# Slot entries of the expert blocks: one load from the DRAM table and an on-chip copy, in place of two loads

## The chip, the cores and the metric

The kernel runs on one core of a Trainium2 chip. The metric is device time in microseconds of one whole execution: one program that computes a decoder layer for a prompt of 1,040 rows and a sample group of 64 rows. Before the change the median of 3 runs is 2792.64 us (2786.09 to 2794.36).

A core has five engines with queues of their own: PE (TensorE, matmuls), DVE (VectorE), ACT (ScalarE), POOL (GpSimd) and SP (SyncE, which only issues DMAs here). They meet through semaphores. DMAs issued by SP travel in queue q1, those issued by POOL (the indirect ones) in queue q0; both are worked off by the same 16 DMA engines.

## The reference

The layer ends in a mixture of experts. That part, cut to what matters:

```python
scores = sigmoid(x @ router_w)
_, idx = top_k(scores + router_bias, 8)              # 8 of 64 experts for each of the 1,104 rows
gate = take(scores, idx); gate = gate / sum(gate) * 2.5
for e in range(64):                                  # rows grouped by expert
    xb = x[rows_of_expert_e]                         # gather
    y = (silu(xb @ w_exp_gate[e]) * (xb @ w_exp_up[e])) @ w_exp_down[e]   # 1024 -> 256 -> 1024
    out[rows_of_expert_e] += y * gate                # scatter with accumulation
```

Everything before it (latent attention, a gated recurrence, the merge, the router, the shared expert) and the final norm are untouched by the change.

## The kernel before, in words

Work is cut into stages; the change lies in `stage_experts`, which fills the last 1,100 us of the run. The router stage has written a table in DRAM: one entry of two words (the row's number and its routing weight) for each slot, 192 slots (`CAP`) to a block. One block is one expert with up to 192 rows; the loop runs over pairs of blocks, s = 0 (called even here) and s = 1 (odd), 64 blocks in all. Nearly every buffer exists twice, one for each s.

For block n each engine does this:

- **SP** loads the entries of a block (`entries`, L1830) and its three weight matrices (`weights`, L1834), gate, up and down, 1 MB each. Everything is loaded two blocks ahead, into the buffers that block n is leaving. A block's entries are loaded twice: into `gi` for block n+2 (L1852), once the gather of block n has landed (L1851), and into `si` for block n itself (L1857), once the scatter of block n-2 has landed (L1856). Between the two stand the weight loads of block n+2, each behind a wait for DVE's `part_weights` of the same matrix of block n (L1854). That of GATE stands near the start of DVE's block n-1, that of UP near its end, that of DOWN at the start of DVE's block n.
- **POOL** gathers rows (`gather`, L1867): two indirect DMAs of 96 rows of 4 KB each, with the row numbers in `gi`; and scatters results (`scatter`, L1875), two indirect DMAs that add into DRAM, with the row numbers in `si`. Its order is: gather n+2, scatter n, gather n+3, wait until scatter n has landed, scatter n+1, wait until scatter n+1 has landed. It signals `si_free` after each of the two landings. So the gather for an even block stands behind the landing of the odd scatter before it; that for an odd block stands behind no landing.
- **ACT** rounds weights and gathered rows to their high parts (L1992, L1997), does the sigmoid, and writes the results scaled by the routing weight (`part`, L1999, which reads `si`; its first part of a block waits for `si`, L2003).
- **DVE** takes the low parts (`part_weights`, L2046 to L2048; `part_quarter`, L2050 to L2053) and does the products of the gate. Its block n begins with `part_weights` of DOWN for block n and of GATE for block n+1.
- **PE** does the gate and up products of block n, then transposes the gathered rows of block n+1 (`turn`, L1907, first transposes of a block wait for `xg_in`, the landed gather) between the down products of block n.

The two places at which the routing data can hold up PE are therefore the transposes of block n+1 (L1916), which need the gathered rows, and the first `part` of block n (L2005), which needs `si`: the down products stop when the banks aren't emptied.

The waits of the functions quoted below decide the order; nothing is planned by a scheduler.

Of the kernel before, what the change touches and what calls it, by code (L numbers as in the profile page):

```python
# [8 lines left out]
I32 = mybir.dt.int32  # L9
# [32 lines left out]
CAP = 192  # L42
HALF = CAP // 2
# [1740 lines left out]
def stage_experts(nc, S, I, O):  # L1784
    arena, split, PS, sem = S.arena, S.split, S.psum, S.sem
# [8 lines left out]
    xr = split.take(2, 2 * KD, HALF)  # L1794
    hr = split.take(2, 2, CAP + 128 - HALF)
    raw_in = [[sem(f"e_{n}{s}") for s in range(2)] for n in ("wg", "wu", "wd")]
    gi_in, si_in, xg_in, y_out = ([sem(f"e_{n}{s}") for s in range(2)] for n in ("gi", "si", "xg", "yo"))
    rounded, parted = ([sem(f"e_{n}{j}") for j in range(3)] for n in ("hi", "lo"))
    xr_full, xr_rounded, xr_parted = sem("e_xrf"), sem("e_xrh"), [sem("e_xrl0"), sem("e_xrl1")]
    gate_full, up_full, sig_ready, gated, h_made, h_ready = (sem("e_" + n) for n in ("gf", "uf", "sg", "gg", "hm", "hr"))  # L1800
    gate_half, up_half, gate_ready, up_ready = (sem("e_" + n) for n in ("gh", "uh", "gr", "ur"))
    part_full, part_copied, zeros = sem("e_pf"), sem("e_pc"), sem("e_zero")
    si_free = [sem("e_sf0"), sem("e_sf1")]
    passed = sem("e_passed")
    GBANK, UBANK, DBANK = (2, 3), (4, 5), (6, 7)
    HI, LO = 0, 1
# [13 lines left out]
    @block.sync  # L1820
    def _(sp):
        last = last_pair(sp)

        def first_slot(n):
            return sp.value_load(S.blocks_i[0:1, 1, bass.ds(n, 1)], min_val=0, max_val=SLOTS - CAP)

        def expert(n):
            return sp.value_load(S.blocks_i[0:1, 0, bass.ds(n, 1)], min_val=0, max_val=EXPERTS - 1)

        def entries(dst, sems, s, first):  # L1830
            sp.dma_start(dst[0:HALF, s].rearrange("p (h w) -> p h w", h=2).bitcast(I32),
                         S.table[bass.ds(first, CAP)].rearrange("(h p) w -> p h w", p=HALF)).then_inc(sems[s], 16)

        def weights(s, j, e):  # L1834
            name = ("w_exp_gate", "w_exp_up", "w_exp_down")[j]
            src = I[name][bass.ds(e, 1)].rearrange("a p n -> p (a n)")
            sp.dma_start(raw[:, s, j], src).then_inc(raw_in[j][s], 16)

        for s in range(2):
            entries(gi, gi_in, s, first_slot(s))  # L1840
        for s in range(2):
            for j in range(3):
                if s == 0 and j == 1:
                    sp.wait_ge(xg_in[0], 32)
                weights(s, j, s)
        with sp.Fori(0, last) as it:
            first = [first_slot(2 * it + s) for s in range(4)]
            e = [expert(2 * it + 2 + s) for s in range(2)]
            for s in range(2):
                n = 2 * it + s  # L1850
                sp.wait_ge(xg_in[s], 32 * (it + 1))  # L1851
                entries(gi, gi_in, s, first[2 + s])  # L1852
                for j in range(3):
                    sp.wait_ge(parted[j], n + 1)  # L1854
                    weights(s, j, e[s])
                sp.wait_ge(si_free[s], it + 1)  # L1856
                entries(si, si_in, s, first[s])  # L1857
        ends = [first_slot(2 * last + s) for s in range(2)]
        for s in range(2):
            sp.wait_ge(si_free[s], last + 1)  # L1860
            entries(si, si_in, s, ends[s])

    @block.gpsimd
    def _(pool):
# [10 lines left out]
        def scatter(s, turn):  # L1875
            if s:
                pool.wait_ge(y_out[0], 32 * (turn + 1))
                pool.sem_inc(si_free[0], 1)
            pool.wait_ge(part_copied, 4 * (2 * turn + s) + 8)
            pool.sem_inc(passed, 1)  # L1880
            for hf in range(2):
                pool.indirect_dma_start(out=S.y_dram, in_=y[0:HALF, s, hf], in_offset=None, compute_op=ALU.add,  # L1882
                                        out_offset=bass.IndirectOffsetOnAxis(ap=si[0:HALF, s, 2 * hf:2 * hf + 1].bitcast(I32), axis=0)
                                        ).then_inc(y_out[s], 16)
# [102 lines left out]
    def _(act):  # L1987
# [11 lines left out]
        def part(s, turn_, p):  # L1999

            hf, c = p // 2, p % 2
            if p == 0:
                act.wait_ge(si_in[s], 16 * (turn_ + 1))  # L2003
            act.wait_ge(part_full, 4 * (2 * turn_ + s) + p + 1)
            act.activation(y[0:HALF, s, hf, 512 * c:512 * (c + 1)], PS[0:HALF, DBANK[c]], ACT.Copy,  # L2005
                           scale=si[0:HALF, s, 2 * hf + 1:2 * hf + 2]).then_inc(part_copied, 1)
# [36 lines left out]
    def _(dve):  # L2043
        last = last_pair(dve)

        def part_weights(s, turn_, j):  # L2046
            dve.wait_ge(rounded[j], 2 * turn_ + s + 1)
            dve.tensor_tensor(wr[:, s, j, LO], raw[:, s, j], wr[:, s, j, HI].bitcast(F32), ALU.subtract).then_inc(parted[j], 1)  # L2048

        def part_quarter(s, turn_, r):  # L2050
            hf, g = r // 2, r % 2
            dve.wait_ge(xr_rounded, 4 * (2 * turn_ + s) + r + 1)
            dve.tensor_tensor(quarter(xr[:, LO], hf, g), bank4(g), quarter(xr[:, HI], hf, g).bitcast(F32), ALU.subtract).then_inc(xr_parted[g], 1)  # L2053

        def body(it, ends):
            for s in range(2):
                n = 2 * it + s
                nxt = (1, it) if s == 0 else (0, it + 1)
                more = not (ends and s)
                part_weights(s, it, DOWN)  # L2060
                if more:
                    part_weights(*nxt, GATE)
# [123 lines left out]
class State:  # L2186
# [11 lines left out]
    def sem(self, name):  # L2198
        self.sems.append(self.nc.alloc_semaphore(name))
        return self.sems[-1]  # L2200
# [176 lines left out]
```

## Time and profile before

| | us |
|---|---|
| median of 3 runs | 2792.64 |
| the profiled execution | 2795.52 |
| its span, first to last instruction | 2793.7 |
| PE busy | 2474.0 (89%) |
| DVE busy | 1362.5 (49%) |
| ACT busy | 1044.8 (37%) |
| POOL busy | 579.3 (21%) |
| q1 (SP's DMAs), share of 16 engines over the span | 27.3% |
| q0 (POOL's DMAs), share of 16 engines over the span | 18.1% |

How to read it: shares over the whole span mix stages with different limits. The stage of the change is read from the slices and timelines of its own stretch, about 1643 to 2730 us. A block of that stage is recognised by one instruction that occurs once in it, the sigmoid (ACT, L2018); the distance of two of them is the block's period. A timeline row gives start, duration, engine, line, operation, output and input, and in brackets the idle time before it with what ended it. A row that ends in x2 merges two instructions: its duration reaches from the start of the first to the end of the second, with the wait between them. GpSimd's rows for an indirect DMA are the time it takes to write and issue it, not the transfer.

### The profile page before, as it was taken

To read this page: it belongs to the slowest core of one execution; us is meant where nothing else is said; L and a number is where in the kernel's file an instruction comes from. 1 tells how busy PE (TensorE), PEld (TensorE's weight loads), DVE (VectorE), ACT (ScalarE), POOL (GpSimd) and SP (SyncE) were. 2 spreads that over 40 slices of the span, in tenths; PEclk is the share of its full clock that TensorE was granted. 3 is DMA by queue.
4 is the path that set the end of the run, shared out by engine and by line. 5 is a ranking of instruction groups with operands and counts; after the bars stand their busy time and mean duration, and the time that the engine had idled before them with its cause. 6 is when DMAs were issued, how large, how long until landed. Compare 5 with 4: busy or idle time off the path is not lost. (4 is left out here: it accounts for less than half of the span.)

```text
span 2793.7 us, 36499 instructions
## 1 busy us (share of the span) xinstructions
PE 2474.0 (89%) x13126; PEld 1851.2 (66%) x13126; DVE 1362.5 (49%) x2701; ACT 1044.8 (37%) x1662; POOL 579.3 (21%) x452
## 2 busy tenths in 40 slices
PE   8888888899966679999998669999999999999990
PEld 4455556564455646666454448999989999989990
DVE  0545544200066601011266137777777777777764
ACT  1145533200023100000021026666666766666652
POOL 0020022000000000000035103344433444344423
PEclk9989989999999889999999889999999999999995
DMA  3000043210010040100113069999999999999964
GB/s 131 0 12 1 1 154 151 87 38 0 0 41 0 0 170 23 45 23 23 51 31 112 15 233 271 287 282 285 287 285 285 298 287 287 273 292 281 284 176 155
DMA packets 113752, 395.23 MB, mean 141 GB/s; under 512 B 41590, under 2 KB 50886, under 8 KB 85254
## 3 DMA queue, kind: packets, MB, share of 16 engines
q1 hardware_dynamic: 78390, 269.63, 27.3%
q0 software_dynamic: 35296, 124.70, 18.1%
q8 instruction: 44, 0.72, 0.1%
q14 instruction: 22, 0.18, 0.0%
HBM read 325.74 MB, written 69.13 MB: 141 GB/s over the span
## 5 line engine op out<-in xcount | busy, mean ns | idle before, releaser
L1934 PE MATMUL banks<-split 128*128 128x384 f32 x1792 | 538.2, 363 | 0.0
L2048 DVE TENSOR_TENSOR split<-rest,split 128x2048 fp32r<-128x2048 f32 x192 | 438.8, 2286 | 108.2 <-ACT split L1992 91.4
L1932 PE MATMUL banks<-split 128*128 128x192 f32 x2048 | 482.7, 256 | 0.0
L1954 PE MATMUL banks<-split 128*128 128x512 f32 x1536 | 406.8, 407 | 17.3 <-ACT rest L2005 14.6
L1932 PEld LDWEIGHTS banks<-split 128*128 128x128 f32 x2048 | 389.1, 192 | 2.7
L1992 ACT CAST split<-rest 128x2048 fp32r<-128x2048 f32 x192 | 359.3, 1904 | 65.0 <-DMA rest<-in_w_exp_gate 60.1
L1393 PE MATMUL banks<-big 128*128 128x368 f32 x1152 | 358.9, 475 | 14.5 <-DMA big<-in_w_merge 14.5
L1934 PEld LDWEIGHTS banks<-split 128*128 128x128 f32 x1792 | 338.9, 189 | 0.0
L1882 POOL DMA_INDIRECT y_rows<-rest x128 | 266.7, 2083 | 336.5 <-ACT rest L2005 299.0
L1954 PEld LDWEIGHTS banks<-split 128*128 128x128 f32 x1536 | 276.5, 190 | 71.9 <-ACT rest L2005 17.5
L1393 PEld LDWEIGHTS banks<-big 128*128 128x128 f32 x1152 | 220.0, 191 | 153.1 <-issue 17.0
L2005 ACT ACTIVATE rest<-banks,rest 96x512 f32<-96x512 f32 x256 | 175.7, 687 | 215.1 <-PE banks L1954 166.2
L1871 POOL DMA_INDIRECT rest<-x_rows,rest x128 | 163.0, 1273 | 414.7 <-issue 298.2
L1486 POOL DMA_INDIRECT slot_table<-big x72 | 69.3, 963 | 526.0 <-DVE big L1648 506.5
L1413 DVE TENSOR_TENSOR big<-big,banks 128x368 f32<-128x368 f32 x24 | 12.9, 537 | 328.0 <-ACT big L1403 328.0
L2053 DVE TENSOR_TENSOR split<-banks,split 128x384 fp32r<-128x384 f32 x256 | 131.5, 550 | 17.8 <-ACT split L1997 17.5
L1402 ACT ACTIVATE big<-banks 128x368 f32<-128x368 f32 x24 | 11.5, 477 | 341.1 <-PE banks L1393 341.1
L177 PE MATMUL banks<-big 128*128 128x368 f32 (+1 forms) x354 | 115.4, 488 | 23.9 <-DMA big<-in_w_cols 13.9
L1916 PE MATMUL banks<-base,rest 96*128 96x96 f32 x1024 | 117.9, 248 | 18.4 <-DMA rest<-x_rows,rest 17.8
L1916 PEld LDWEIGHTS banks<-base,rest 96*128 96x128 f32 x1024 | 106.9, 142 | 40.1 <-DMA rest<-x_rows,rest 17.7
L995 PE MATMUL banks<-big 128*128 128x368 f32 x384 | 121.4, 480 | 7.7 <-DMA big<-in_w_cols 7.7
L1499 PE MATMUL banks<-big 128*128 128x512 f32 (+1 forms) x288 | 125.3, 594 | 2.9 <-PEq L2220 2.9
(327 smaller groups left out, 3088.0 us busy)
## 6 DMA issues: line engine op xcount, KB each, us to landing
rest<-in_w_exp_gate SPq DMA_DIRECT2D x64, 1024.0 KB, 9.1
rest<-in_w_exp_up SPq DMA_DIRECT2D x64, 1024.0 KB
rest<-in_w_exp_down SPq DMA_DIRECT2D x64, 1024.0 KB, 7.1
big<-in_w_merge SPq DMA_DIRECT2D x8, 1536.0 KB, 6.3
big<-in_w_cols SPq DMA_DIRECT2D x11, 512.0 KB, 3.8
x_rows<-big SPq DMA_DIRECT2D x9, 512.0 KB
y_rows<-big SPq DMA_DIRECT2D x9, 512.0 KB, 2.6
big<-in_x_cols SPq DMA_DIRECT2D x3, 1472.0 KB, 17.7
```

The source lines that it names most:

```text
L1393: ins = pe.matmul(PS[:, 4 * (u % 2) + b, 0:CH], w[:, s, at + j], src[:, j, cols], start=(j == 0), stop=(j == k - 1))
L1499: ins = pe.matmul(PS[0:r, 2 * (i % 2) + c], S.merged[:, k, 128 * i:128 * i + r], wout[:, k, 512 * c:512 * (c + 1)], start=(k == 0), stop=( ...
L1871: pool.indirect_dma_start(out=xg[0:HALF, s, hf], out_offset=None, in_=S.x1_dram, in_offset=bass.IndirectOffsetOnAxis(ap=gi[0:HALF, s, 2 * ...
L1882: pool.indirect_dma_start(out=S.y_dram, in_=y[0:HALF, s, hf], in_offset=None, compute_op=ALU.add, out_offset=bass.IndirectOffsetOnAxis(ap= ...
L1916: ins = pe.transpose(PS[:, g, HALF * k:HALF * (k + 1)], xg[0:HALF, s, hf, 512 * g + 128 * k:512 * g + 128 * (k + 1)], S.ident[0:HALF, 0:HALF])
L1932: ins = pe.matmul(PS[:, banks[f], 0:CAP], wr[:, s, j, LO, at:at + 128], x[:, k, 0:2], start=False, stop=False)
L1934: ins = pe.matmul(PS[:, banks[f], 0:2 * CAP], wr[:, s, j, HI, at:at + 128], x[:, k], start=False, stop=(k == KD - 1))
L1954: ins = pe.matmul(PS[:, DBANK[c]], hr[:, a, f, HALF * hf:HALF * hf + 128], wr[:, s, DOWN, b, at:at + 512], start=(f == 0 and j == 0), stop ...
L1992: act.copy(wr[:, s, j, HI], raw[:, s, j]).then_inc(rounded[j], 1)
L2005: act.activation(y[0:HALF, s, hf, 512 * c:512 * (c + 1)], PS[0:HALF, DBANK[c]], ACT.Copy, scale=si[0:HALF, s, 2 * hf + 1:2 * hf + 2]).then ...
L2048: dve.tensor_tensor(wr[:, s, j, LO], raw[:, s, j], wr[:, s, j, HI].bitcast(F32), ALU.subtract).then_inc(parted[j], 1)
L2053: dve.tensor_tensor(quarter(xr[:, LO], hf, g), bank4(g), quarter(xr[:, HI], hf, g).bitcast(F32), ALU.subtract).then_inc(xr_parted[g], 1)
```

## The change

The second load of the entries, with its semaphores `si_in`, goes: 64 loads inside the loop and after it. In its place DVE copies `gi` to `si` (`keep_entries`), two copies of 96x2 words (row numbers as integers, routing weights as floats), at the start of its block n, ahead of `part_weights` of DOWN. The copies wait until the gather of block n has landed and until `si_free` says that the scatter of block n-2 has. They signal `si_made`. SP's load of the next entries into `gi` now waits for `si_made` of block n in place of `xg_in`, since the copy reads `gi`. ACT's first part and POOL's scatter wait for `si_made` as well.

```diff
             for s in range(2):
                 n = 2 * it + s
-                sp.wait_ge(xg_in[s], 32 * (it + 1))
-                entries(gi, gi_in, s, first[2 + s])
+                sp.wait_ge(si_made[s], 2 * (it + 1))
+                entries(s, first[s])
                 for j in range(3):
                     sp.wait_ge(parted[j], n + 1)
                     weights(s, j, e[s])
-                sp.wait_ge(si_free[s], it + 1)
-                entries(si, si_in, s, first[s])
-        ends = [first_slot(2 * last + s) for s in range(2)]
-        for s in range(2):
-            sp.wait_ge(si_free[s], last + 1)
-            entries(si, si_in, s, ends[s])
...
         def scatter(s, turn):
             if s:
                 pool.wait_ge(y_out[0], 32 * (turn + 1))
                 pool.sem_inc(si_free[0], 1)
+            pool.wait_ge(si_made[s], 2 * (turn + 1))
             pool.wait_ge(part_copied, 4 * (2 * turn + s) + 8)
...
             if p == 0:
-                act.wait_ge(si_in[s], 16 * (turn_ + 1))
+                act.wait_ge(si_made[s], 2 * (turn_ + 1))
...
+        def keep_entries(s, turn_):
+            dve.wait_ge(xg_in[s], 32 * (turn_ + 1))
+            dve.wait_ge(si_free[s], turn_ + 1)
+            kept, loaded = (v[0:HALF, s].rearrange("p (h w) -> p h w", h=2) for v in (si, gi))
+            dve.tensor_copy(kept[:, :, 0].bitcast(I32), loaded[:, :, 0].bitcast(I32)).then_inc(si_made[s], 1)
+            dve.tensor_copy(kept[:, :, 1], loaded[:, :, 1]).then_inc(si_made[s], 1)
+
         def body(it, ends):
             for s in range(2):
                 n = 2 * it + s
                 nxt = (1, it) if s == 0 else (0, it + 1)
                 more = not (ends and s)
+                keep_entries(s, it)
                 part_weights(s, it, DOWN)
```

What stands in SP's queue for one block of the loop, before the change (L1831 is the load of entries, first into `gi`, last into `si`; ISA and REGISTER_ALU rows compute addresses and wait values):

```order
L1851 ISA
L1831 ISA
L1831 DMA rest<-slot_table 96x2x2
L1854 REGISTER_ALU
L1837 ISA
L1837 DMA rest<-in_w_exp_gate 128x2048
L1837 DMA rest<-in_w_exp_up 128x2048
L1837 DMA rest<-in_w_exp_down 128x2048
L1831 ISA
L1831 DMA rest<-slot_table 96x2x2
```

And with it:

```order
L1851 ISA
L1831 ISA
L1831 DMA rest<-slot_table 96x2x2
L1854 REGISTER_ALU
L1837 ISA
L1837 DMA rest<-in_w_exp_gate 128x2048
L1837 DMA rest<-in_w_exp_up 128x2048
L1837 DMA rest<-in_w_exp_down 128x2048
```

The last load is gone; the three weight loads keep their place behind the first load of entries, whose wait (L1851) is now one for DVE.

DVE's queue from the end of one block (`part_quarter`, `part_weights` UP) into the next (`part_weights` DOWN and GATE, then the products of the gate), before:

```order
L2053 TENSOR_TENSOR split<-banks,split 128x384
L2048 TENSOR_TENSOR split<-rest,split 128x2048
L2047 ISA
L2048 TENSOR_TENSOR split<-rest,split 128x2048
L2064 TENSOR_TENSOR rest<-rest,banks 128x384
```

And with the change (the lines behind it have moved on by numbers only: L2053 is now L2048, L2048 is L2043, L2064 is L2067):

```order
L2048 TENSOR_TENSOR split<-banks,split 128x384
L2054 COPY rest<-rest 96x2
L2055 COPY rest<-rest 96x2
L2043 TENSOR_TENSOR split<-rest,split 128x2048
L2042 ISA
L2043 TENSOR_TENSOR split<-rest,split 128x2048
L2067 TENSOR_TENSOR rest<-rest,banks 128x384
```

Two copies stand between the blocks, ahead of both weight parts.

## Rows read from the trace of the kernel before

**Rows 1.** The page, parts 1 and 2: busy time of the engines, DMA share by slice.

```profile
PE 2474.0 (89%) x13126; PEld 1851.2 (66%) x13126; DVE 1362.5 (49%) x2701; ACT 1044.8 (37%) x1662; POOL 579.3 (21%) x452
...
DMA  3000043210010040100113069999999999999964
```

**Rows 2.** Waits, 1200 to 2750 us: who waited for whom, total, times, longest us.

```profile
ACT rest L2005 <- DMA rest<-slot_table: 48.8, 16, 5.0
...
PE banks L1916 <- DMA rest<-x_rows,rest: 17.8, 5, 16.8
```

**Rows 3.** Timeline of ScalarE: start us, duration us, group, [idle before <- releaser].

```profile
1672.37 0.52 ACT L2018 ACTIVATE rest<-rest 128x384 f32<-128x384 f32 x1 [0.62 <-issue]
...
2072.58 0.53 ACT L2018 ACTIVATE rest<-rest 128x384 f32<-128x384 f32 x1 [0.62 <-DVE rest L2064]
...
2080.53 0.68 ACT L2005 ACTIVATE rest<-banks,rest 96x512 f32<-96x512 f32 x1 [3.24 <-DMA rest<-slot_table]
...
2090.08 0.53 ACT L2018 ACTIVATE rest<-rest 128x384 f32<-128x384 f32 x1 [0.62 <-DVE rest L2064]
...
2106.29 0.53 ACT L2018 ACTIVATE rest<-rest 128x384 f32<-128x384 f32 x1 [0.62 <-DVE rest L2064]
...
2715.76 0.53 ACT L2018 ACTIVATE rest<-rest 128x384 f32<-128x384 f32 x1 [0.62 <-DVE rest L2064]
```

**Rows 4.** Windows, the stretch 1700 to 2700 us: busy by engine, PEclk, DMA share, GB/s.

```profile
1700.00:2700.00 1000.00, 986.15 (x6296) 911.72 (x6295) 750.66 (x1026) 686.76 (x908) 410.29 (x241) 1.00 0.95 283
```

**Rows 5.** Timeline of SyncE's queue, one odd block (start us, duration us).

```profile
2114.74 0.35 SPq L1837 DMA_DIRECT2D rest<-in_w_exp_up  x1
2117.87 0.33 SPq L1837 DMA_DIRECT2D rest<-in_w_exp_down  x1
2118.39 7.22 SPq L1831 DMA_DIRECT2D rest<-slot_table  x2
2126.02 0.19 SPq L1837 DMA_DIRECT2D rest<-in_w_exp_gate  x1
```

**Rows 6.** Timeline of GpSimd, around the same pair, and one earlier gather.

```profile
2049.71 2.65 POOL L1871 DMA_INDIRECT rest<-x_rows,rest  x1 [9.28 <-issue]
...
2102.09 1.47 POOL L1882 DMA_INDIRECT y_rows<-rest  x1 [8.84 <-ACT rest L2005]
2103.86 2.88 POOL L1882 DMA_INDIRECT y_rows<-rest  x1 [0.30 <-issue]
2115.39 0.94 POOL L1871 DMA_INDIRECT rest<-x_rows,rest  x1 [8.65 <-issue]
2116.64 2.01 POOL L1871 DMA_INDIRECT rest<-x_rows,rest  x1 [0.30 <-issue]
```

**Rows 7.** Timeline of TensorE: the first transposes in that odd block.

```profile
2125.83 0.82 PE L1916 MATMUL banks<-base,rest 96*128 96x96 f32 x8
```

**Rows 8.** DMA view, 2114 to 2150 us in 40 slices of 0.9 us.

```profile
GB/s 0 55 91 437 419 337 346 373 419 323 287 246 205 201 214 237 351 256 228 214 369 378 401 437 400 428 437 392 205 205 366 364 350 296 228 0 0 55 127 391
```

**Rows 9.** Timeline of VectorE: the two weight parts at a block's start.

```profile
2115.56 2.28 DVE L2048 TENSOR_TENSOR split<-rest,split 128x2048 fp32r<-128x2048 f32 x1
2119.32 2.29 DVE L2048 TENSOR_TENSOR split<-rest,split 128x2048 fp32r<-128x2048 f32 x1 [1.47 <-ACT split L1992]
```

**Rows 10.** Groups by line and form, VectorE: a small integer copy in SBUF.

```profile
L1646 DVE COPY big<-big 128x8 int32<-128x8 int32 x8 | 1.3, 167 | 0.0
```

**Rows 11.** Line 1882 (scatter), 2000 to 2200 us: from issue to landing.

```profile
DMA to landing us min/median/max: 7.2/9.2/10.8
```

**Rows 12.** DMA queues, 1674 to 1678 us: packets, MB, share of 16 engines.

```profile
q1 hardware_dynamic: 137, 0.89, 66.7%
q0 software_dynamic: 120, 0.45, 34.7%
```

**Rows 13.** DMA queues, 2120 to 2122.5 us.

```profile
q1 hardware_dynamic: 107, 0.88, 91.9%
q0 software_dynamic: 32, 0.07, 10.7%
```

More of the change, by code:

```diff
@@ L1796, in stage_experts @@
     raw_in = [[sem(f"e_{n}{s}") for s in range(2)] for n in ("wg", "wu", "wd")]
-    gi_in, si_in, xg_in, y_out = ([sem(f"e_{n}{s}") for s in range(2)] for n in ("gi", "si", "xg", "yo"))
+    gi_in, xg_in, y_out = ([sem(f"e_{n}{s}") for s in range(2)] for n in ("gi", "xg", "yo"))
     rounded, parted = ([sem(f"e_{n}{j}") for j in range(3)] for n in ("hi", "lo"))
@@ L1802, in stage_experts @@
     part_full, part_copied, zeros = sem("e_pf"), sem("e_pc"), sem("e_zero")
-    si_free = [sem("e_sf0"), sem("e_sf1")]
+    si_free, si_made = [sem("e_sf0"), sem("e_sf1")], [sem("e_sm0"), sem("e_sm1")]
     passed = sem("e_passed")
@@ L1828, in expert, with entries @@
             return sp.value_load(S.blocks_i[0:1, 0, bass.ds(n, 1)], min_val=0, max_val=EXPERTS - 1)
-        def entries(dst, sems, s, first):
-            sp.dma_start(dst[0:HALF, s].rearrange("p (h w) -> p h w", h=2).bitcast(I32),
-                         S.table[bass.ds(first, CAP)].rearrange("(h p) w -> p h w", p=HALF)).then_inc(sems[s], 16)
+        def entries(s, first):
+            sp.dma_start(gi[0:HALF, s].rearrange("p (h w) -> p h w", h=2).bitcast(I32),
+                         S.table[bass.ds(first, CAP)].rearrange("(h p) w -> p h w", p=HALF)).then_inc(gi_in[s], 16)
         def weights(s, j, e):
@@ L1839, in _ @@
         for s in range(2):
-            entries(gi, gi_in, s, first_slot(s))
+            entries(s, first_slot(s))
         for s in range(2):
@@ L1846, in _ @@
         with sp.Fori(0, last) as it:
-            first = [first_slot(2 * it + s) for s in range(4)]
+            first = [first_slot(2 * it + 2 + s) for s in range(2)]
             e = [expert(2 * it + 2 + s) for s in range(2)]
```

## The prediction

> **What bounds the kernel now.** I read the page first: PE is busy 89% of the span, and in the last third of the slices the DMA engines stand at 9 of 10 as well [rows 1]. So the expert stage has two candidates, and an average does not choose between them. Next the period of a block, from the sigmoid that occurs once in each. The 64 blocks lie between 1672.37 and 2715.76: 63 periods in 1043.4 us, 16.56 each. An undisturbed period is 2106.29 - 2090.08 = 16.21 [rows 3], and in such a one PE has no gap. 63 x 16.21 is 1021.2, so all stalls of the stage together cost 22.2 us. That is the most the change can win in the loop.
>
> The waits name what makes them. ACT's first part waited for the slot entries 16 times, 48.8 us; PE's transposes waited for gathered rows 5 times, 17.8 us, of which 16.8 is the first gather of the stage [rows 2]. The first is what a long block looks like: at 2080.53 ACT had waited 3.24 us for `si`, and that period is 17.50 [rows 3]. ACT idles there some 1.6 us anyway for PE's down products, which is why 48.8 us of waiting are only about 20 us of delay: 22.2 less the 2 that I give to late gathers (1.0 on PE's own row, the rest is what the late rows did to ACT and DVE behind it, an estimate).
>
> Last, the share of the DMA engines over a thousand microseconds of the stage: 0.95 [rows 4]. There is next to no slack in transfers either, so it matters which one stands ahead of which.
>
> **What goes.** The load of `si` stood last in q1, behind three weight loads; with the copy the entries are on chip before the block begins. That takes the 16 waits: -20 us. The load itself is 192 entries of 8 bytes; SP needs about 0.4 us to issue it and is not the bound. No term.
>
> **What is added.** Two DVE copies of 96x2 words. The nearest row is an integer copy of 128x8 in 167 ns [rows 10]: 0.33 us a block. DVE idles 1.47 us before the second weight part of each block, waiting for ACT [rows 9], which covers them: 0. Without cover it would be 64 x 0.33 = 21 us. The new wait for `si_free` stands on DVE with everything of the block behind it. The scatter that it waits for landed at latest just before the gather at 2115.39 [rows 6], DVE comes at 2115.56 [rows 9]: 0.2 us to spare, while landing takes 7.2 to 10.8 us [rows 11]. Up to 1.47 us late is swallowed by the same idle time. I take 0 and keep what lies beyond it as a rival.
>
> **What is moved, and the term that decides.** In SP's queue the gate and up loads stand behind the load into `gi`, and that now waits for DVE's start of block n. Both parts they also wait for (GATE and UP of block n) are done by then, so SP issues entries, gate and up in one go. Before, the gate load of the odd block's queue came at 2126.02 and that of the even one earlier in its block; now it comes together with up, just where up alone stood. Nothing that needs these weights suffers: ACT rounds them a whole block (16 us) later, and at 437 GB/s [rows 8] 1 MB takes 2.4 us.
>
> But look at what else is issued there. The gather for the next even block stands behind the landing of the odd scatter and goes out at 2115.39 and 2116.64 (the second half until 2118.65) [rows 6]. It is back at about 2125.2: SP's pair of entry loads ends at 2125.61 [rows 5], and the second of them waited for it. PE wants the rows at 2125.83 [rows 7]. The margin is 0.6 us in an undisturbed pair; it is this kernel's second critical path, with nothing to show for itself but those few waits of [rows 2].
>
> Now the engines' work in that gap. Before: up (issued 2114.74, first bytes a good microsecond later, done about 2118.3 [rows 5, 8]), first half, down (2117.87), second half. That down goes ahead of the second half is in 2120 to 2122.5: 91.9% for q1, 10.7% for q0 [rows 13]. Changed: DVE is through the copies at 2115.9, SP issues entries at 2116.0, gate at 2116.5, up at 2117.0; gate's bytes run from 2117.7 to 2120.1. The first half comes behind gate instead of behind up, 1.8 us later, and the second behind up instead of down. So the rows land 1.8 us later, less the margin: PE stalls 1.2 us in each pair. If instead gather and weights share packet by packet from 2118.3 on, the 192 packets of 4 KB pass with as many of 8 KB beside them: 1.57 MB at 437 GB/s are 3.6 us, 0.79 MB at 356 (the slice of rows 8 in which weights and rows are mixed) are 2.2, end at 2124.1. Counted in the same way, before ended at 2115.9 + 2 x 2.4 + 2.2 = 2122.9 and landed 2.3 later; with 1.2 to 2.3 for that the rows land at 2125.3 to 2126.4, and the stall is 0 to 0.6. That both queues run at once does occur: 66.7% and 34.7% between 1674 and 1678 [rows 12], with a deep backlog in q1. Bounds 0 and 1.2; I take 0.8, nearer the upper since the order in rows 13 is from the very place.
>
> The Trainium skill, DMA: Bandwidth & Descriptors, section Queues, rings and completion order, says that each DMA engine "round-robins between the queue rows it has work for, at packet granularity". By that the gather gets in after at most one packet of weights and never stands behind the whole backlog; rows 12 agree, and rows 13 show that the turn can be as long as one weight load. Without the rule, first come first served, the stall would be that of the last rival below.
>
> In some pairs it is worse. In 10 of 30 pairs the first half of the even gather takes 2.4 to 3.0 us to issue in place of 0.94, as at 2049.71 [rows 6]: it starts after DVE's long subtraction has begun and ends after it. Then both halves come some 2 us later. Before, they found the queue nearly empty; now gate and up are both in front, and rows 13's order makes it 1.8 to 2.5 us more on a margin that is already gone. I take 2.2, bounds 1.8 and 2.6.
>
> The Trainium skill, SBUF — State Buffer, section Who interferes with whom, has the reason: a DVE instruction with two SBUF inputs contends with a GpSimd one that reads SBUF, and who issues first holds the port for the whole instruction. The 2.65 us against 0.94 agree. The copies move the subtraction 0.3 us back, which by that rule would let a few more first halves through; it is not counted.
>
> The sum over 31 pairs: 2/3 x 0.8 + 1/3 x 2.2 = 1.27 us, times 31 = 39 us. These stalls include what late gathers cost now, so the stage goes from 22.2 us of stalls to 39: +17. The profiled execution took 2795.52, 2.9 over the median; the difference goes on the median: 2792.64 + 17 = 2810.
>
> **Rivals.** *The wait goes and nothing takes its place.* For it: the gather shares the engines packet by packet; the gate load no longer runs between the two halves of the odd scatter, which might land, and so start the gather, a microsecond earlier. Against: weights issued before that scatter fill the same place. Stalls fall to 0 to 3 us: 2792.6 - 20 = 2773. It decides if the gather lands before 2125.8 on the clock of the rows, that is loses less than 0.6 us.
>
> *The gain is handed back evenly:* 0.7 us a pair, 22 us: 2793. This is the case between, where the rows land 1 us later in the plain pairs and the late third loses little more.
>
> *DVE's new wait becomes the chain.* Three weight loads and the even scatter share the engines, the scatter lands more than 1.5 us after DVE's arrival and DVE drags the gate products. For it: 0.2 us to spare. Against: where PE already stalls for the gather, the scatter gains the same time. With 3 us late in every second block, 1.5 on the path: 31 x 1.5 = 47 on top of the 39, less 22: 2857.
>
> *First come, first served:* the second half behind gate, up and down, 2117.7 + 3 x 2.4 + 2.2 = 2127.1 and 1.2 to land, 2128.3, 2.5 us too late in each pair: 78 - 22 = +56: 2849.
>
> *The change doesn't do what it says:* only if `si_free` came so late that entries are again last. Then the stall sits on DVE, which is the third case.
>
> **How the numbers follow.** Late gathers, net loss: 0.42, centre 2810, its own range 2798 to 2830. Wait gone, no new one: 0.33, 2773. Even: 0.15, 2793. DVE's chain 0.05, first come first served 0.05. About 0.3% (8 us) is what a measurement of this kernel can tell from no change. Faster by more than that: 0.35; within: 0.17; slower: 0.48. The range has to take in most of the second case, whose end is 2771, and the upper half of the first with the 2.6 of the late pairs: 2771 to 2840.
>
> **What would show it.** Right: no wait of ACT L2005 for entries; SP's entries, gate and up within 1.5 us of each other at each block start; PE L1916 waiting for gathered rows in most odd blocks, about 1 us each and 30 to 40 us in all; even blocks at 16.2. Wrong: L1916 waits of under 10 us in total (then the second case), or a DVE copy idle for more than 1.5 us before it with gate products late (the DVE case). If the period of the undisturbed pair itself changed, some engine's cost was missed.

## The result: 3.7% slower, and the profile after

| us | before | after |
|---|---|---|
| median (6 runs each) | 2790.32 | 2893.45 |
| lowest to highest | 2782.00 to 2794.36 | 2882.04 to 2898.45 |
| ratio after/before, 95% interval | | 1.0369 [1.0344, 1.0394] |
| span of the profiled execution | 2793.7 | 2887.3 |

The forecast was 2810 with a range up to 2840. The direction, slower, came true; the size did not: +103 us, not +17.

The page after, parts 1 and 2, the rows that answer to [rows 1]:

```profile
PE 2505.3 (87%) x13126; PEld 1874.9 (65%) x13126; DVE 1378.2 (48%) x2829; ACT 1048.6 (36%) x1662; POOL 587.1 (20%) x452
...
DMA  3000042200100310101130488888888888888764
```

PE's work is the same 13126 instructions, yet it is busy 31 us longer. The DMA digits of the expert stage fell from 9 to 8: the transfers of the stage are spread over more time.

Waits of after, 1200 to 2950 us (total, times, longest), the rows that answer to [rows 2]:

```profile
PE banks L1911 <- DMA rest<-x_rows,rest: 100.5, 31, 16.2
...
DVE rest L2054 <- POOLq L1872: 6.5, 13, 0.6
```

ACT's wait for `slot_table` is not in the list any more (48.8 us in [rows 2]). PE's wait for gathered rows, 17.8 us over 5 times before, is 100.5 us over 31. L1911 is the line of the transposes now. The second row is the copies' wait for `si_free`.

ScalarE after: the sigmoid that opens the measure of the stage, a plain even block, a long odd one, a plain even one, a short odd one, and the last, to be laid beside [rows 3]:

```profile
1664.66 0.52 ACT L2013 ACTIVATE rest<-rest 128x384 f32<-128x384 f32 x1 [0.62 <-DVE rest L2067]
...
2131.52 0.53 ACT L2013 ACTIVATE rest<-rest 128x384 f32<-128x384 f32 x1 [0.62 <-DVE rest L2067]
...
2147.73 0.53 ACT L2013 ACTIVATE rest<-rest 128x384 f32<-128x384 f32 x1 [0.62 <-DVE rest L2067]
...
2155.97 0.48 ACT L1992 CAST split<-banks 128x384 fp32r<-128x384 f32 x1 [4.40 <-PE banks L1911]
...
2169.85 0.53 ACT L2013 ACTIVATE rest<-rest 128x384 f32<-128x384 f32 x1 [0.62 <-DVE rest L2067]
...
2186.06 0.53 ACT L2013 ACTIVATE rest<-rest 128x384 f32<-128x384 f32 x1 [0.62 <-DVE rest L2067]
...
2191.19 0.86 ACT L1992 CAST split<-banks 128x384 fp32r<-128x384 f32 x2 [1.28 <-PE banks L1911]
...
2809.73 0.53 ACT L2013 ACTIVATE rest<-rest 128x384 f32<-128x384 f32 x1 [0.62 <-DVE rest L2067]
```

From the first to the last sigmoid it is 1145.1 us, against 1043.4 before. 63 undisturbed periods are still 1021.2, so the stalls grew from 22.2 to 123.9 us: +101.7, and nothing outside the stage grew (it begins 7.7 us earlier in this execution of after; the first sigmoid of the kernels below lies anywhere from 1659 to 1679). The even period is 2147.73 - 2131.52 = 16.21. The odd one that follows is 22.12, with ACT idle for 4.40 us because the transposes had not filled its banks.

I split blocks 2 to 63 (counted from 0) by their period, each sigmoid less 5.78 us, which puts a block's edge near its start. All even ones take 16.2. Of the 30 odd ones from block 3 to 61, 17 are long (21.95 to 23.98, mean 22.66) and 13 short (17.09 to 17.65, mean 17.30). The long ones carry 17 x 6.45 = 110 us, the short ones 13 x 1.09 = 14. Every short one follows a long one, and all but three of the long ones after the first follow a short one.

SyncE's queue after, at the start of the long block and of the short one (to be laid beside [rows 5]):

```profile
2141.16 0.33 SPq L1831 DMA_DIRECT2D rest<-slot_table  x1
2141.74 0.33 SPq L1837 DMA_DIRECT2D rest<-in_w_exp_gate  x1
...
2143.22 0.33 SPq L1837 DMA_DIRECT2D rest<-in_w_exp_down  x1
...
2179.49 0.33 SPq L1831 DMA_DIRECT2D rest<-slot_table  x1
2180.07 0.33 SPq L1837 DMA_DIRECT2D rest<-in_w_exp_gate  x1
...
2181.55 0.33 SPq L1837 DMA_DIRECT2D rest<-in_w_exp_down  x1
```

Entries, gate, up (between the two rows of L1837) and down, 3 MB, leave within 2.1 us, where [rows 5] had up, down and gate 3 and 8 us apart. GpSimd over the same two pairs (beside [rows 6]):

```profile
2141.77 2.24 POOL L1865 DMA_INDIRECT rest<-x_rows,rest  x1 [9.81 <-issue]
2144.32 0.93 POOL L1865 DMA_INDIRECT rest<-x_rows,rest  x1 [0.30 <-issue]
...
2178.98 0.94 POOL L1865 DMA_INDIRECT rest<-x_rows,rest  x1 [8.71 <-issue]
2180.23 2.11 POOL L1865 DMA_INDIRECT rest<-x_rows,rest  x1 [0.30 <-issue]
```

The first two rows are the even gather of the long pair: it starts at 2141.77, after SP has issued gate, and takes 2.24 us for its first half. In the short pair it starts at 2178.98, before SP has issued anything, and its first half takes 0.94.

TensorE in the long block, first transposes (beside [rows 7]):

```profile
2155.31 1.26 PE L1911 MATMUL banks<-base,rest 96*128 96x96 f32 x8 [4.10 <-DMA rest<-x_rows,rest]
```

The DMA queues of after from 2146 to 2151 us, and from 2151 to 2155:

```profile
q1 hardware_dynamic: 187, 1.36, 75.1%
q0 software_dynamic: 117, 0.42, 25.1%
...
q0 software_dynamic: 156, 0.57, 53.8%
q1 hardware_dynamic: 95, 0.65, 51.3%
```

The gather's 192 packets run from 2147.3 to 2154.4, beside the backlog of weights. Sorted by microsecond, the trace's packet records show 26 to 32 row packets and 18 to 29 of weights in most of them, packet for packet. Behind the weights, at 2158, 84 row packets (those of the next gather) pass in one. The 192 packets of the gather take 7.1 us. In the ten pairs of before whose first half was held, with at most 12 packets of weights left beside them, 192 rows took 2.8 to 3.0 us.

The gather also starts late behind the weights. The queues from 2144 to 2147 us, just after its first half has left GpSimd in the long pair, and from 2180.6 to 2182 in the short pair:

```profile
q1 hardware_dynamic: 168, 1.25, 99.1%
...
q0 software_dynamic: 70, 0.28, 82.3%
```

In the long pair the first row packet comes 3.3 us after the end of that issue, while weights alone pass; in the short pair, where no weights are on their way yet, 0.7 us after it. By the packet records it is 3.1 to 3.4 us in all 17 long pairs, behind 157 to 176 packets of weights, and 0.7 to 0.8 in the 13 short ones.

Windows after, two pairs of blocks and then the idle of the long block (each engine's busy us and count in the order PE, PEld, DVE, ACT, POOL; granted clock; DMA share; GB/s):

```profile
2125.70:2141.90 16.20, 16.20 (x106) 15.04 (x105) 12.77 (x20) 11.40 (x15) 4.47 (x3) 1.00 0.81 251
2141.90:2164.10 22.20, 18.10 (x106) 16.37 (x105) 13.29 (x20) 11.43 (x15) 9.33 (x6) 0.92 0.82 248
2164.10:2180.30 16.20, 16.20 (x105) 15.03 (x105) 12.12 (x20) 11.39 (x15) 5.35 (x4) 1.00 0.78 243
2180.30:2197.80 17.50, 16.44 (x106) 15.03 (x105) 12.52 (x20) 11.35 (x15) 7.71 (x5) 1.00 1.00 305
...
2151.00:2156.00 5.00, 0.90 (x8) 0.70 (x7) 1.34 (x4) 0.42 (x3) 1.45 (x2) 0.97 1.05 285
2156.00:2160.00 4.00, 4.00 (x17) 3.24 (x16) 3.31 (x3) 0.94 (x3) 0.00 (x0) 0.62 1.04 263
2160.00:2164.00 4.00, 4.00 (x23) 3.29 (x22) 2.50 (x5) 2.72 (x5) 0.00 (x0) 1.00 0.12 28
```

The long block is 6.0 us longer than the plain one. 4.10 of it is PE's idle time; the other 1.90 is PE's own work, 18.10 us for matmuls that take 16.20 otherwise: in the 4 us after the idle the granted clock is 0.62, a mean of the two levels 1.2 and 2.4 GHz. After the idle of the short block, 1.1 us, the clock stays at 1.00. The DMA engines, full at 2151 to 2160, are all but empty at 2160 to 2164 (0.12): the transfers of a block come in one heap.

### The profile page after: what moved, and what is told of

It reads as the page before. It is cut to its first block and busy times, and to the rows that moved or that the text cites. A ratio compares the mean times of both kernels' runs of the same rounds, so it can differ in the third digit from the quotient of the medians.

```text
span 2887.3 us, 36338 instructions
## 1 busy us (share of the span) xinstructions
PE 2505.3 (87%) x13126; PEld 1874.9 (65%) x13126; DVE 1378.2 (48%) x2829; ACT 1048.6 (36%) x1662; POOL 587.1 (20%) x452
## 5 line engine op out<-in xcount | busy, mean ns | idle before, releaser
L2043 DVE TENSOR_TENSOR split<-rest,split 128x2048 fp32r<-128x2048 f32 x192 | 439.0, 2286 | 98.1 <-ACT split L1987 98.1
L1949 PE MATMUL banks<-split 128*128 128x512 f32 x1536 | 429.9, 425 | 2.5 <-DVE split L2075 2.4
L1927 PEld LDWEIGHTS banks<-split 128*128 128x128 f32 x2048 | 389.2, 192 | 2.7
L1393 PE MATMUL banks<-big 128*128 128x368 f32 x1152 | 358.4, 474 | 15.5 <-DMA big<-in_w_merge 15.5
L1929 PEld LDWEIGHTS banks<-split 128*128 128x128 f32 x1792 | 339.0, 189 | 0.0
L1949 PEld LDWEIGHTS banks<-split 128*128 128x128 f32 x1536 | 294.1, 202 | 60.1 <-DVE split L2075 2.8
L1865 POOL DMA_INDIRECT rest<-x_rows,rest x128 | 172.4, 1347 | 415.1 <-issue 299.5
L1911 PE MATMUL banks<-base,rest 96*128 96x96 f32 x1024 | 128.8, 263 | 101.0 <-DMA rest<-x_rows,rest 100.5
L1911 PEld LDWEIGHTS banks<-base,rest 96*128 96x128 f32 x1024 | 113.6, 151 | 128.5 <-issue 93.1
L2048 DVE TENSOR_TENSOR split<-banks,split 128x384 fp32r<-128x384 f32 x256 | 134.5, 551 | 106.5 <-ACT split L1992 104.9
L1992 ACT CAST split<-banks 128x384 fp32r<-128x384 f32 x256 | 116.3, 474 | 100.5 <-PE banks L1911 99.9
```

What stands on the lines that cost most here:

```text
L1393: ins = pe.matmul(PS[:, 4 * (u % 2) + b, 0:CH], w[:, s, at + j], src[:, j, cols], start=(j == 0), stop=(j == k - 1))
L1865: pool.indirect_dma_start(out=xg[0:HALF, s, hf], out_offset=None, in_=S.x1_dram, in_offset=bass.IndirectOffsetOnAxis(ap=gi[0:HALF, s, 2 * ...
L1911: ins = pe.transpose(PS[:, g, HALF * k:HALF * (k + 1)], xg[0:HALF, s, hf, 512 * g + 128 * k:512 * g + 128 * (k + 1)], S.ident[0:HALF, 0:HALF])
L1927: ins = pe.matmul(PS[:, banks[f], 0:CAP], wr[:, s, j, LO, at:at + 128], x[:, k, 0:2], start=False, stop=False)
L1929: ins = pe.matmul(PS[:, banks[f], 0:2 * CAP], wr[:, s, j, HI, at:at + 128], x[:, k], start=False, stop=(k == KD - 1))
L1949: ins = pe.matmul(PS[:, DBANK[c]], hr[:, a, f, HALF * hf:HALF * hf + 128], wr[:, s, DOWN, b, at:at + 512], start=(f == 0 and j == 0), stop ...
```

## The experiments

The stage is always the stretch from its first to its last sigmoid (1043.4 before, 1145.1 after). "Row waits" are those of PE's transposes for gathered rows.

### e1: the copies stay, entries go third

```diff
-                sp.wait_ge(si_made[s], 2 * (it + 1))
-                entries(s, first[s])
                 for j in range(3):
+                    if j == DOWN:
+                        sp.wait_ge(si_made[s], 2 * (it + 1))
+                        entries(s, first[s])
                     sp.wait_ge(parted[j], n + 1)
```

> The changed kernel, with SyncE's order inside a block altered: gate and up loads first, each behind its own old wait, then the load of entries behind the copies, then down. The copies on DVE and their waits stay. Theory A (the gather for the even block shares the DMA engines with gate and up, issued together just before it): up goes out again at 14.2 us of a block and gate near 5, the gather lands as in the kernel before, PE waits under 10 us for rows in the loop, no wait for entries: 2765 to 2785 us, faster than before. Theory B (the copies and the wait for si_free in DVE's queue make the loss): DVE's queue is untouched, so it stays near 2890. Theory C (the load of entries itself comes too late for the gather that needs it): it comes even later here, so 2890 or more, with GpSimd waiting for slot_table.

2780.73 us, ratio to before 0.9968 [0.9952, 0.9984]; stage 1032.3.

```profile
PE banks L1912 <- DMA rest<-x_rows,rest: 21.8, 8, 16.7
```

The copies and DVE's new wait are all still here, and the loss is gone: it is the order in SP's queue. With gate and up back at their old places the change is a small gain. The even gather starts late here as well, in 17 of 30 pairs later than 15.1 us of its even block, as in this one (16.1 us):

```profile
2064.61 2.16 POOL L1866 DMA_INDIRECT rest<-x_rows,rest  x1 [9.92 <-issue]
```

Yet the odd block behind this one takes 16.31, and 14 of the 17 take 16.2 to 16.7 (the others 17.2, 17.3 and 20.0). With gate and up through before it, a late gather alone does not make a long block.

### e2: the kernel before, its gate load held back to the up load's place

```diff
-                    sp.wait_ge(parted[j], n + 1)
+                    sp.wait_ge(parted[UP if j == GATE else j], n + 1)
```

> The kernel before, two loads of entries, no copies; only SyncE's gate load waits for DVE's low part of UP in place of that of GATE, so gate and up go out together at the end of a block. Theory A: most of the loss is here without any copy: long waits of PE for gathered rows in odd blocks, half-speed clock behind the longest, 2850 to 2900 us, and the waits for entries remain or vanish in them. Theory B and theory C: near 2790.

2896.16, ratio 1.0400 [1.0365, 1.0435]; stage 1150.1.

```profile
ACT rest L2005 <- DMA rest<-slot_table: 149.4, 32, 5.7
...
PE banks L1916 <- DMA rest<-x_rows,rest: 26.2, 11, 15.6
```

The loss is as large, but by another way: `si`, still loaded last, is late in every second block, and the row waits hardly grow. So it shows that a heap of loads costs whoever stands behind it, and says little on the gather.

### e5: e1 with the gate load beside the up load

The same edit of the wait as in e2, in e1.

> As e1_entries_third (copies, entries loaded third, 2780.7 us), but the gate load waits for DVE's low part of UP, so gate goes out with up at 14.3 us of a block instead of at 5. The only difference to e1 is when 1 MB is issued. Theory A (bytes of weights beside the gather and the scatter that it follows): PE waits for gathered rows in all odd blocks, 2870 to 2900 us. Rival D (the changed kernel lost by loading up 1 to 2 us later, behind DVE's copies, not by the gate load): up is as early as in the kernel before, so 2780 to 2795 us.

2817.68, ratio 1.0096 [1.0072, 1.0120]; stage 1076.2; row waits 47.5 us, 13 times. That lies between what the two theories gave. Gate's place alone makes 44 us of stage against e1. The rest to after (69 us) comes with the entries in front of gate and up, which puts both behind DVE's copy and so beside the even gather.

### e4: the copies behind part_weights of DOWN

```diff
-                keep_entries(s, it)
                 part_weights(s, it, DOWN)
+                keep_entries(s, it)
```

> The changed kernel, with the copies one instruction later on DVE, behind the low part of DOWN. All three weight loads then go out together at about 1.4 us of a block, 2.5 us later than in the changed kernel, and the even gather gets ahead of them. Theory A: the gather lands in time, PE's waits for rows fall below 20 us, 2765 to 2800 us, unless the three loads now hold up the scatter, which the next gather stands behind. Theory B (DVE's copies and wait are the cost): the wait for si_free is 2.5 us shorter, gain of the 6 us that DVE waits for it at most: 2885. Theory C: the entries come 2.5 us later still: 2890 or more.

2918.71, ratio 1.0468 [1.0437, 1.0499]; stage 1173.4; row waits 115.8 us, 31 times. I was wrong, and the caveat in the text came true. From issue to landing of the scatters, 2000 to 2300 us, before ([rows 11] is the same line over a shorter stretch), after, e1 and e4:

```profile
DMA to landing us min/median/max: 7.2/9.5/10.8
```

```profile
DMA to landing us min/median/max: 9.7/10.6/12.5
```

```profile
DMA to landing us min/median/max: 6.5/9.6/11.8
```

```profile
DMA to landing us min/median/max: 10.1/12.3/12.7
```

The heap now runs beside the odd scatter, whose landing starts the even gather; that start moves to 0.9 us into the odd block, and the odd blocks take 21.1 to 21.8, all but three of them. This half of the matter was not in my sum: the weights delay the gather's start as well as its packets.

### e3 and e11: what GpSimd's long issue costs

e3 splits the subtraction of DOWN into two halves of 1.21 us, back to back:

```diff
+            if j == DOWN:
+                dve.tensor_tensor(wr[:, s, j, LO, 0:DM], raw[:, s, j, 0:DM], wr[:, s, j, HI, 0:DM].bitcast(F32), ALU.subtract)
+                dve.tensor_tensor(wr[:, s, j, LO, DM:], raw[:, s, j, DM:], wr[:, s, j, HI, DM:].bitcast(F32), ALU.subtract).then_inc(parted[j], 1)
+                return
```

> The changed kernel, with DVE's low part of DOWN as two subtractions of 1024 columns. In 16 of 31 pairs the first half of the even gather takes 2.2 to 3.0 us to issue, held by the single subtraction of 2.28 us. If that hold is what turns a stall of 1 us into one of 4.5 (theory A with the hold on the shared port as its amplifier), it ends up to 1.1 us earlier, the long pairs get shorter by 1 to 2 us or fewer: 2850 to 2878 us. If the hold doesn't matter and only the bytes ahead of the gather do: 2890 within 5 us. Two instructions cost DVE some 0.06 us more, which no theory counts.

2890.12, ratio 1.0372 [1.0339, 1.0404]; stage 1137.8; row waits 96.5 us. The first halves of the long pairs were still held 2.2 to 3.3 us, until the second subtraction ended: GpSimd did not get in between the two. It tells nothing on what the hold costs. e11 does, with zeros written in place of DOWN's low part (so the down product lacks that part's share):

```diff
+            if j == DOWN:
+                dve.memset(wr[:, s, j, LO].bitcast(F32), 0.0).then_inc(parted[j], 1)
+                return
```

> The changed kernel, with DVE writing zeros in place of the low part of DOWN (this part of the computation is left out): no second input from SBUF while GpSimd issues the even gather. Every wait stays. If the hold of GpSimd by that subtraction makes the long pairs: first halves take 0.94 us throughout, the 4.5 us waits of PE give way to those of 1 us, 2800 to 2850 us. If it only goes along with a gather that is late anyway: 2880 to 2900 us with GpSimd's rows short. If GpSimd's rows stay at 2 to 3 us, zeros hold it as well and this run tells nothing.

2876.85, ratio 1.0279 [1.0261, 1.0296]; stage 1129.2; row waits 89.3 us, 30 times. GpSimd's gathers in e11, long pair and short pair, and TensorE's first transposes in the same two:

```profile
2143.15 0.94 POOL L1865 DMA_INDIRECT rest<-x_rows,rest  x1 [9.57 <-issue]
2144.39 0.93 POOL L1865 DMA_INDIRECT rest<-x_rows,rest  x1 [0.30 <-issue]
...
2178.83 0.94 POOL L1865 DMA_INDIRECT rest<-x_rows,rest  x1 [8.53 <-issue]
2180.08 0.93 POOL L1865 DMA_INDIRECT rest<-x_rows,rest  x1 [0.30 <-issue]
```

```profile
2155.35 0.88 PE L1911 MATMUL banks<-base,rest 96*128 96x96 f32 x8 [2.52 <-DMA rest<-x_rows,rest]
...
2189.93 0.88 PE L1911 MATMUL banks<-base,rest 96*128 96x96 f32 x8 [0.37 <-DMA rest<-x_rows,rest]
```

No first half is held (0.94), and the pair in which the gather starts late still stalls: 2.52 us, against 0.37 where it starts early. The hold goes along with lateness; the long blocks come without it, 15 of them here, of 22.2 us in the mean. The stage is 16 us shorter than after's, so the hold, or the shorter instruction on DVE, may still be worth that much; I expected 2880 to 2900 for a hold that does not matter.

### e6: the gate load cut to an eighth

```diff
-        def weights(s, j, e):
+        def weights(s, j, e, first_load=False):
...
-            sp.dma_start(raw[:, s, j], src).then_inc(raw_in[j][s], 16)
+            cut = DEXP if j == GATE and not first_load else 2 * DM
+            sp.dma_start(raw[:, s, j, 0:cut], src[:, 0:cut]).then_inc(raw_in[j][s], 16)
```

The first loads, ahead of the loop, are whole; later blocks use seven eighths of stale gate weights.

> The changed kernel, with only an eighth of each gate matrix loaded in the loop (256 of 2048 columns; the rest keeps the first two experts' values, so this part of the computation is left out). Issue times and waits stay, 0.9 MB a block go. Theory A: the even gather has 8 packets less per engine beside it, lands 2 us or more earlier, PE's waits for rows are nearly gone: 2765 to 2785 us. Rival E (what costs is the order of issue and the waits, not bytes): 2880 to 2893 us.

2869.82, ratio 1.0290 [1.0272, 1.0308]; stage 1123.8; row waits 89.2 us, 31 times. Wrong again: I had thought that gate's bytes in front were the price. The gather starts 1.4 us earlier in its block than in after's short pairs (13.4 us against about 14.9); but its second half then falls on the subtraction, as GpSimd shows, and is out no sooner than there (18.3 us of the block in both), and up and down are still there beside the rows:

```profile
2135.78 1.57 POOL L1866 DMA_INDIRECT rest<-x_rows,rest  x1 [7.21 <-PE banks L1912]
2137.66 2.95 POOL L1866 DMA_INDIRECT rest<-x_rows,rest  x1 [0.30 <-issue]
```

The odd blocks take 18.0 to 21.1 us now: less far apart, none as long as after's.

### e9: gate where e1 has it, up behind the entries

```diff
                 for j in range(3):
-                    if j == DOWN:
+                    if j == UP:
                         sp.wait_ge(si_made[s], 2 * (it + 1))
                         entries(s, first[s])
```

> Copies as in the changed kernel. SyncE's order: gate (at 5 us of a block, its old wait), entries behind the copies, up, down. So gate is early and up late by 1.8 us: the fourth corner beside e1 (both early, 2781), e5 (gate late, up at 14.8, 2818) and the changed kernel (both late, 2893). If the loss is bytes that run beside the even gather, up alone, issued at 16.0, runs beside both halves where in e1 it is through before them: PE waits for rows about 1 to 3 us in odd blocks, 2825 to 2870 us. If it needs the whole 3 MB bunch: 2781 to 2795 us.

2950.29, ratio 1.0540 [1.0522, 1.0557]; stage 1194.1; row waits 130.1 us, 31 times. This was to be between e1 and after, and is the slowest of all. Gate lies at 5.0 us of the block, between the halves of the odd scatter, as in e1; what differs from e1 is that up is late. The scatters of 2000 to 2300 us land after 11.2 us in the median, against 9.6 in e1, and the even gather, which starts when the odd scatter has landed, never starts early (15.5 us of its even block or later; 15.8 and 16.1 here):

```profile
2142.48 2.52 POOL L1866 DMA_INDIRECT rest<-x_rows,rest  x1 [9.55 <-issue]
...
2182.76 2.17 POOL L1866 DMA_INDIRECT rest<-x_rows,rest  x1 [9.90 <-issue]
```

So the loss is not a sum of bytes in front of the rows. As I read it, what counts is when the odd scatter lands, relative to the heap; why this order is worse than after's was not tested further.

### e7, e8, e10: the gather freed from the landing

GpSimd gathers for the next even block first and only then waits for the odd scatter (the first pair is written out ahead of the loop, since it has no scatter to wait for):

```diff
                     gather(s, it + 1)
+                if s == 0 and not first:
+                    pool.wait_ge(y_out[1], 32 * it)
+                    pool.sem_inc(si_free[1], 1)
                 scatter(s, it)
-            pool.wait_ge(y_out[1], 32 * (it + 1))
-            pool.sem_inc(si_free[1], 1)
```

e7 is after with it, e8 is e1 with it, e10 is before with it.

> The changed kernel, with GpSimd gathering for the next even block before it waits for the landing of the odd scatter (the wait and its si_free signal come behind the gather). Weights stay bunched, every byte stays. If the loss needs the chain odd scatter landed, even gather, PE's transposes, it is gone with its first link: the gather has 9 us more, PE waits for rows under 10 us in the loop, 2765 to 2780 us. If bunched weights cost in another way (scatter landing late, copies waiting for si_free, late down weights): 2800 us or more, with DVE waiting for GpSimd's signal in its profile.

> e1_entries_third and the free gather of e7 together: weights spread as in the kernel before, no chain. All stalls of the stage should be gone but for the first block: the stage at 64 x 16.21 us, 2766 to 2775 us. If it comes out equal to e7, spreading the loads is worth nothing once the gather is free.

> The kernel before (two loads of entries, no copies) with the even gather issued ahead of the wait for the odd scatter's landing. What the change is worth with the chain out of play is this kernel against e7 (2766.5). If the 20 us of waits for entries stay as they were: 2783 to 2790 us, PE's waits for rows gone, ACT's waits for entries some 50 us. If the gather, now in another place beside the entries' load, makes them land later: up to 2800; if earlier: down to 2775.

| | median us | ratio to before | stage us | row waits |
|---|---|---|---|---|
| e7 (after) | 2766.54 | 0.9915 [0.9898, 0.9932] | 1021.2 | 16.8, once |
| e8 (e1) | 2764.86 | 0.9917 [0.9898, 0.9936] | 1020.9 | 16.9, once |
| e10 (before) | 2783.90 | 0.9946 [0.9929, 0.9963] | 1033.5 | 16.8, once |

The waits of e7 and of e10:

```profile
PE banks L1914 <- DMA rest<-x_rows,rest: 16.8, 1, 16.8
```

```profile
ACT rest L2008 <- DMA rest<-slot_table: 33.3, 12, 5.2
```

e7's stretch from 1750 to 2650 us by windows (beside [rows 4]):

```profile
1750.00:2650.00 900.00, 900.00 (x5772) 834.72 (x5772) 696.43 (x1061) 630.62 (x835) 356.21 (x222) 1.00 0.94 291
```

The loads still leave in one heap in e7, SP's queue is that of after, and not one block is longer than 16.21: PE is busy 900.00 of 900 us. Spreading the loads (e8) adds nothing then. That shows the chain: the heap hurts only through odd scatter landed, even gather, transposes. How much of it is the late start and how much the sharing, e7 does not separate, since its gather, at 6.5 us into the block, is clear of both. e1 says that the late start alone, without the heap beside it, costs little. And e7 against e10 is the change alone with that chain out of play: 12.3 us less of stage, for the 12 entry waits that e10 still has; by the two ratios to before it is 0.3%, some 9 us, give or take 7. e7 and e8 beat both kernels.

## Why the prediction was right and wrong

**What bounds the kernel: right.** PE with an undisturbed pair of 16.21 us a block, 22.2 us of stalls, two chains of the routing data behind it. The second one, with its margin of 0.6 us, is what decided.

**The gain, 20 us for the entry waits: right in kind, smaller in size.** The waits are gone in after. Measured alone (e7 against e10, one trace each) it is 12.3 us of stage, with 33.3 us of such waits left in e10 where before had 48.8.

**The copies and DVE's wait, 0: right.** e7 and e8 have them, and no block of theirs is over its 16.2 us; DVE's wait for `si_free` was 0.6 us at most in after.

**Entries, gate and up in one go: right, and down with them.** The margin lost in plain pairs, 0.8 us, is right too: 1.09 in the 13 short blocks.

**The step that failed: the late pairs.** The prediction had them so: in 10 of 30 the first half is held by the subtraction, and "rows 13's order makes it 1.8 to 2.5 us more on a margin that is already gone. I take 2.2, bounds 1.8 and 2.6." Both factors were wrong. With the measured ones in place of 1/3 x 2.2, 17 x 6.45 + 13 x 1.09 is 124 us, where 39 stood. What is in the 6.45:

- 4.1 us of idle time on PE's own row in the pair shown. A gather that starts when all three matrices stand in q1 gets its first packet 3.3 us after the issue and then shares the engines packet for packet with what is left of the 3 MB: 7.1 us for its packets, with 181 of weights beside them. From the end of the last issue to the last row packet it is 8.8 us, where the plain pair of [rows 6] took 5.6. The second half is out at 19.5 us of the block in place of 18.1. Together 4.6 us later, less the margin of 0.6, that is about the 4.1. The prediction let the rows of the late pairs stand behind gate and up and then run freely. It did have the sharing case, with 192 packets of weights beside the rows, and gave it 3.6 + 2.2 = 5.8 us from mean rates of bytes; but it used that only for the lower bound of the plain pairs. In the trace the two kinds of packet cost more together than one after the other: one of weights took 0.31 us by itself (2144 to 2147 us) and 0.40 beside rows.
- 1.9 us of slower work in the same pair, with the granted clock at 0.62 in the 4 us after the idle. PE's busy time rose by 31 us in all (2474.0 to 2505.3), nearly a third of the loss, with the same instructions, and e7, which has no such idles, is back at 2468.7. None of my terms had it: I took the cost of an idle PE to be the idle time.

**And the share of late pairs, 1/3 held constant, looks like a feedback.** A short odd block leaves SP's loads of the even block some 0.6 us later against PE. The odd scatter then shares with them and lands later, the gather for the next even block starts at 15.1 to 16.0 us of this one, in place of 14.8 to 14.9, and the odd block behind it is long; the length gives the scatter the time back, and the next is short again. That fits 14 of the 17: in the other three, which follow a long block, the loads have not moved (down at 0.93 us of the block) and the gather still starts at 15.1 to 15.3. That blocks and starts go together so, 17 of 17 and 13 of 13, is read from the trace. That this landing is a link of the chain is shown by e7, where it no longer matters; in e4 and e9 the gather starts late in all pairs from block 3 on and none is short. The heap beside the rows is the other link: e1's late gathers, without it, cost little. The step from the 0.6 us to the later landing was not tested by itself.

**The reason given for late pairs** (the port that DVE and GpSimd contend for, from the Trainium skill, SBUF — State Buffer, Who interferes with whom) holds for the issue: with a memset, which reads nothing, no first half is held (e11). It is not what costs most: e11's late pairs stall all the same, and of the 102 us that the stage lost, at most 16 go with it. I had taken a sign of lateness for its cause.

**The rivals.** "Nothing takes its place" (2773, 0.33) fell, though e7 shows that it is what the change does once the gather is free. DVE's chain (2857) and first come, first served (2849) came nearest in time, and neither is what happens: DVE waits 6.5 us in all, and the rows do not stand behind the whole backlog. Nor do they get in at once, as the prediction had it: the first of them came behind 157 to 176 packets of weights of the 384. The rule of the Trainium skill, DMA: Bandwidth & Descriptors, Queues, rings and completion order, that an engine goes round its queues at packet granularity, agrees with the packet records here from the first row packet on, one for one. The late entry of that packet, and the sharing behind it for as long as the backlog lasts, were what was dear.

## What to carry to other kernels

Before a transfer is moved or an issue delayed, list what else is in flight at the new time, and follow each chain through it that has less than a microsecond of slack, back to what starts it: a heap of loads delays both the start of a dependent gather and its packets. Such a chain shows in the profile only as a few waits of a few us; and once it breaks, PE's idle time is followed by a slower clock (here behind 2.6 and 4.1 us of it). The better repair was not to place the loads well but to take the landing wait out of the gather's way: -0.9%, whatever the order of the loads.

## What the runs showed of the hardware that was not expected

- Two queues with deep backlogs, weights of 8 KB and rows of 4 KB a packet, advance one packet for one: 26 to 32 row packets in most microseconds beside weights, up to 84 alone.
- The first packet of an indirect gather came 0.7 us after its issue ended where no weights were on their way, and 3.1 to 3.4 us after it in the 17 long pairs, beside weights. Why so long is not shown.
- Two back-to-back subtractions of 1.21 us on VectorE hold an indirect gather on GpSimd as one of 2.28 does (2.2 to 3.3 us for an issue of 0.94); a memset of 1.76 us in its place does not.
- After 4.1 us without matmuls, TensorE's granted clock was 0.62 over the next 4 us, between 1.2 and 2.4 GHz; after 2.6 us in e6 it was the same, as its windows show; after the 1.1 us of after's short block it stayed at 1.00.

```profile
2147.00:2150.40 3.40, 0.82 (x6) 0.56 (x4) 1.70 (x5) 1.00 (x2) 0.52 (x1) 1.00 1.03 258
2150.40:2154.40 4.00, 3.99 (x16) 3.28 (x17) 2.89 (x3) 0.86 (x2) 0.00 (x0) 0.62 1.03 253
```
